# In the mixer of a two-layer transformer block, VectorE's normalisation of the attention probabilities moves in front of the low half of the weights

## The chip, the cores and the metric

The kernel runs on one core of one Trainium2 chip. The metric is the device time of one execution in microseconds (us); of several executions the median is given.

## The reference

Two blocks are computed one after the other for 256 tokens of width 2048, all in float32. The first block is a hybrid mixer (pooling, forgetting attention, a gated linear recurrence) and a gated feed-forward part, both modulated by a conditioning vector. The second block has two layers, and the change is in these. A layer is:

```python
h = rmsnorm_2(x, norm_mix[l]);  proj = h @ w_in[l]          # 2048 -> 4352: q, k, v of three kinds
oa = window_attention(...)         # 8 heads "A", bias from a table, a sink
ob = neighborhood_attention(...)   # 8 heads "B", bias, column mask
oc = axial_global_attention(...)   # 16 heads "C", rotary, normalised q and k
mix = concatenate([rmsnorm_2(oa, ga), rmsnorm_2(ob, gb), rmsnorm_2(oc, gc)])
x = x + mix @ w_o[l]
u = relu(rmsnorm_2(x, norm_mlp[l]) @ w_up[l]);  x = x + (u * u) @ w_down[l]
```

In every head, `p = softmax(s)` over 256 keys and `o = p @ v`, for 256 queries and a head width of 64.

## The kernel before

**Weights in pieces.** All weights come as pieces of 512 rows by 512 columns (1 MB), 536 of them in the program, into a ring of four buffers. A float32 product is made of three products of rounded parts, so each piece goes through three hands: SyncE loads it into `raw` (`load`, L590), ScalarE rounds it into `w_hi` (`hi`, L2216 to L2218), VectorE makes the remainder `w_lo = raw - w_hi` (`lo`, L1263 to L1266). TensorE then does 48 matmuls of 256 columns on it (`piece`, L700, matmuls at L695). SyncE's load of a piece waits until TensorE has finished the piece four before (`pe_done`).

**One program of pieces.** In a layer of the second block, pieces 0 to 31 are `w_in`, 32 to 47 are `w_o`, and then comes the feed-forward part. Each engine has a loop over the pieces of its own, and a table of hooks: work that the engine does at a given piece, in the order in which it was registered. VectorE's loop is at L2112 to L2115: at step p it first makes `w_lo` of piece p + 1, then runs the hooks of p. ScalarE's loop casts `w_hi` of piece p + 1 at its step p and then runs its hooks. TensorE executes piece p and then its hooks of p. Semaphores tie the engines together. Each engine executes in order.

**Attention beside the pieces.** The 32 heads of a layer are spread over hooks by `head_slots` (L135 to L153), which gives for each p from 12 to 40 three lists of heads: those whose probabilities are transposed, those whose output is then computed, and those whose scores are computed. TensorE does all three as its hook of p (`slot`, L920; transposes at L698 in `turn`, in `finish`, L847, which waits for `p_done`). Starts are at 12, 14, ... 25, 27 (B4, B5), 29 (B6, B7), 31 (B0, B1), 33 (B2, B3), 34 (A0, A1), 36 (A2, A3), 38 (A4, A5), 39 (A6, A7); the first head of a pair is transposed at p + 1, the second at p + 2, or both at p + 1 where the next start follows directly.

On VectorE the same table is registered twice, at L2076 for the heads whose probabilities are due (`probs`, L1635: the reciprocal at L1648 and two multiplications at L1652, for A heads an addition at L1641 before them) and at L2082 for new heads (`row_max`, L1655: bias at L1677, mask at L1681, maximum at L1685 or L1687). Both are hooks of p + 1, so TensorE's transposes in its hook of p wait for VectorE's step p + 1. ScalarE computes the exponentials (`exps`, L2424) in its step p + 2 of the start and copies the transposed probabilities out of PSUM (L2389).

Other work of VectorE in this part: evacuations of projected tiles (`evac2`, L2020), sums of squares for the group norms (`fold`, L1317), reciprocal roots (`rsqrt`, L1271 to L1301), the norms (`group_norm`, L1993, and `group_lo`, L2002) and the residual sums (`add_plain`, L2007). GpSimd loads the bias tiles (L2789, L2795) into four buffers, each when the head four before has used its own.

Of the kernel before, what the change touches and what calls it, by code (L numbers as in the profile page):

```python
# [50 lines left out]
HEADS1 = 8  # L51
# [147 lines left out]
def width2(p):  # L199

    return 256 if p < 4 * len(IN2) and IN2[p // 4] == 7 else PIECE_N
# [52 lines left out]
HEADS2 = 32  # L254


def two_stage_kernel(nc, a, stage=9):

    with ExitStack() as ctx:
# [973 lines left out]
        def _(dve):  # L1233
# [4 lines left out]
            def hook(p, fn, *args):  # L1238
                hooks.setdefault(p, []).append((fn, args))

            def run_hooks(p):
                for fn, args in hooks.pop(p, []):
                    fn(*args)
# [19 lines left out]
            def lo(quad, j, n=PIECE_N):  # L1263
                dve.wait_ge(hi_done, quad * 4 + (j + 1))
                m = PIECE_K * n
                v.tensor_tensor(w_lo[j][:, 0:m], raw[j][:, 0:PIECE_K * n], w_hi[j][:, 0:m], ALU.subtract).then_inc(lo_done, 1)  # L1266
# [37 lines left out]
            def fold(bufs, start, sems, lo=0, hi=5, count=folded):  # L1304

                n = start + lo
                if lo == 0:
                    dve.wait_ge(*sems[0])
                acc = bufs[0]
                parts = [(acc[:, :, :], b[:, :, :], w) for b, w in zip(bufs[1:], sems[1:])]  # L1310
                parts += [(acc[:, 0:2, :], acc[:, 2:4, :], None), (acc[:, 0, :], acc[:, 1, :], None)]
                for k, (a_, b_, w) in list(enumerate(parts))[lo:hi]:
                    if w is not None:
                        dve.wait_ge(*w)
                    if k:
                        dve.wait_ge(count, n)
                    v.tensor_tensor(a_, a_, b_, ALU.add).then_inc(count, 1)  # L1317
                    n = n + 1
# [316 lines left out]
            def probs(H, kind, h, no):  # L1635

                b = H % 2
                dve.wait_ge(exp_done, no + 1)
                if kind == "A":
                    n = lay[0] * 40 + (HEADS1 + 24 + 2 * (H - 24))  # L1640
                    v.tensor_tensor(rsum[:, b, :], rsum[:, b, :], sink_e[:, b, :], ALU.add).then_inc(rcp_done, 1)  # L1641
                    dve.wait_ge(rcp_done, n + 1)
                    n = n + 2
                elif kind == "F":
                    n = H + 1
                else:
                    n = lay[0] * 40 + (HEADS1 + H + 1)
                v.reciprocal(rinv[:, b, :], rsum[:, b, :]).then_inc(rcp_done, 1)  # L1648
                dve.wait_ge(rcp_done, n)
                for t in range(QT):  # L1650
                    w = P * (t + 1) if kind == "F" else T
                    i = v.tensor_scalar(s_sb[b][:, t, 0:w], s_sb[b][:, t, 0:w], rinv[:, b, t:t + 1], None, ALU.mult)  # L1652
                i.then_inc(p_done, 1)
# [43 lines left out]
            def slot(done, new, base):  # L1697
                for H, kind, h in done:
                    probs(H, kind, h, base + H)
                for H, kind, h in new:  # L1700
                    row_max(H, kind, h, base + H)
# [217 lines left out]
            if stage >= 3:  # L1919
                mb = MISC_B  # L1920
                for l in range(LAYERS):
# [127 lines left out]
                    def fold_f(lo_, hi_):  # L2049
                        fold(sq_x, 0, [(sq_f, q + 1) for q in range(4)], lo_, hi_, folded_f)  # L2050

                    for q in range(1, 4):
                        hook(q - 1, split_lo, q, q, LC_MIX, nb)
                    fb = l * FOLD_L + FOLD_L0
# [19 lines left out]
                    for z in (24, 25):  # L2074
                        hook(Q_ALT_AT + 1, q_end, z)
                    for p, (done, _, _) in SLOTS2.items():  # L2076
                        hook(p + 1, slot, done, [], l * HEADS2 + HEADS1)
                    for z, p in Q_ROT_AT.items():
                        hook(p + 1, q_end, z)
                    for b_ in (1, 2):  # L2080
# [29 lines left out]
                    hook(52, read_rstd, "mlp")  # L2110

                    for p in range(48):  # L2112
                        if p:
                            lo(lq + (p + 1) // 4, (p + 1) % 4, width2(p + 1))
                        run_hooks(p)  # L2115
# [75 lines left out]
        def _(act):  # L2191
# [248 lines left out]
            for p, (_, _, new) in SLOTS1.items():  # L2440
                hook(p + 2, exps, new, 0)
            for p, (trans, _, _) in SLOTS1.items():
                hook(p + 1, copy_probs, trans, 0)
# [14 lines left out]
            for p, (_, outs, _) in SLOTS1.items():  # L2458
                hook(p + 1, copy_out, outs)
# [366 lines left out]
```

## Time and profile before

| | |
|---|---|
| median of 3 runs | 3362.93 us (3355.77 to 3363.58) |
| the profiled execution | 3361.67 us, span 3360.0 us |
| TensorE matmuls | busy 3233.0 us, 96% of the span |
| VectorE | busy 2225.3 us, 66% |
| ScalarE | busy 1420.0 us, 42% |
| mean granted TensorE clock | 0.972 |

The span is the time from the first to the last instruction in the profile; the device time has 1.67 us around it. In the names of engines, PE is TensorE, PEld its weight loads, DVE is VectorE, ACT is ScalarE, POOL is GpSimd and SP is SyncE. "G" and "Dn" are the accumulators in PSUM; scores, transposes and small products use the buffers of Dn. `s_sb` holds a head's scores and then its probabilities. Pieces 28 to 41, where the change works, lie at about 1426 to 1556 us of the span in layer 0 and at about 2478 to 2606 us in layer 1.

### The profile page before, as it was taken

What the parts mean: (1) busy time and instruction counts of PE and PEld (TensorE: products, weight loads), DVE (VectorE), ACT (ScalarE), POOL (GpSimd) and SP (SyncE); (2) the same over time, 40 slices, a digit from 0 to 9 for tenths busy, and PEclk for the clock granted to TensorE, in tenths of its full rate; (3) what the DMA queues carried; (4) which work ended last, traced back from release to release, by engine and by line L of the source; (5) the groups of instructions that cost most, each with busy time, mean ns of one, the idle gap of its engine ahead of it and who ended that gap; (6) DMA issues with size and microseconds to landing.
All of it is one profiled execution on the core that took longest, in us unless ns stands there. A gap on an engine that the chain in (4) does not pass through costs nothing.

```text
span 3360.0 us, 62992 instructions
## 1 busy us (share of the span) xinstructions
PE 3233.0 (96%) x27070; PEld 3157.3 (94%) x27070; DVE 2225.3 (66%) x2257; ACT 1420.0 (42%) x1384; POOL 158.1 (5%) x292
## 2 busy tenths in 40 slices
PE   5999979999999999989999999999999999999998
PEld 5988879999999999978999999999987999999998
DVE  5788877665666677677655555657667755555655
ACT  3243334444444444545433434334455434334333
POOL 2111100000000100011000000000010000000000
PEclk6899989999999999999999999999999999999999
DMA  9788867666666645445555555555444565555553
GB/s 385 283 307 310 293 256 253 220 211 213 208 204 205 220 151 164 140 138 163 188 195 192 192 195 189 198 189 175 139 138 139 176 197 190 194 193 190 197 189 136
DMA packets 320748, 681.66 MB, mean 203 GB/s; under 512 B 14769, under 2 KB 21621, under 8 KB 320165
## 3 DMA queue, kind: packets, MB, share of 16 engines
q1 hardware_dynamic: 286272, 562.74, 50.6%
q0 software_dynamic: 31232, 109.07, 8.9%
q10 hardware_dynamic: 3108, 7.89, 0.6%
q8 instruction: 104, 1.70, 0.2%
q14 instruction: 32, 0.25, 0.0%
HBM read 677.47 MB, written 7.94 MB: 204 GB/s over the span
## 4 chain that ended last, share of the span: by engine, by line
PE 84%; DVE 9%; DMA 3%; issue 2%; ACT 2%; POOL 0%; ACTq 0%; DVEq 0%; POOLq 0%; SPq 0%
PE G L695 51%; PE Dn L695 32%; DVE w_lo L1266 2%; DVE ada_acc L1393 1%; PE Dn L698 1%; DMA ada_raw<-in_w_ada 1%; DMA raw<-in_w_in 1%; DMA zT<-in_w_ada 1%; ACT w_hi L2218 1%; DVE sq L1317 1%; DMA raw<-in_w_out 0%; DVE s_sb L1677 0%; DVE sq L1993 0%; DVE s_sb L1681 0%; DVE s_sb L1652 0%
## 5 line engine op out<-in xcount | busy, mean ns | idle before, releaser
L2218 ACT CAST w_hi<-raw 128x2048 fp32r<-128x2048 f32 (+2 forms) x536 | 1017.3, 1900 | 1427.7 <-DMA raw<-in_w_down 428.6
L1266 DVE TENSOR_TENSOR w_lo<-raw,w_hi 128x2048 fp32r<-128x2048 f32 (+2 forms) x536 | 1219.4, 2275 | 603.0 <-ACT w_hi L2218 602.2
L695 PE MATMUL G<-h_hi,w_hi 128*128 128x256 f32 x5632 | 1583.5, 281 | 10.5 <-DVE w_lo L1266 6.3
L695 PE MATMUL G<-h_lo,w_hi 128*128 128x256 f32 x5632 | 1572.1, 279 | 0.0
L695 PE MATMUL G<-h_hi,w_lo 128*128 128x256 f32 x5632 | 1571.4, 279 | 0.0
L695 PEld LDWEIGHTS G<-h_hi,w_hi 128*128 128x128 f32 x5632 | 1071.2, 190 | 25.1 <-issue 20.8
L695 PEld LDWEIGHTS G<-h_lo,w_hi 128*128 128x128 f32 x5632 | 1071.4, 190 | 0.2
L695 PEld LDWEIGHTS G<-h_hi,w_lo 128*128 128x128 f32 x5632 | 1071.2, 190 | 0.0
L695 PE MATMUL Dn<-act_hi,w_hi 128*128 128x256 f32 x2752 | 763.0, 277 | 7.4 <-DVE act_lo L1811 7.4
L695 PE MATMUL Dn<-act_hi,w_lo 128*128 128x256 f32 x2752 | 762.5, 277 | 0.0
L695 PE MATMUL Dn<-act_lo,w_hi 128*128 128x256 f32 x2752 | 762.4, 277 | 0.0
L695 PEld LDWEIGHTS Dn<-act_hi,w_hi 128*128 128x128 f32 x2752 | 519.6, 189 | 7.9 <-DVE act_lo L1811 7.9
L695 PEld LDWEIGHTS Dn<-act_lo,w_hi 128*128 128x128 f32 x2752 | 519.4, 189 | 0.0
L695 PEld LDWEIGHTS Dn<-act_hi,w_lo 128*128 128x128 f32 x2752 | 519.3, 189 | 0.0
L2007 DVE TENSOR_TENSOR xT<-xT,Dn 128x1024 f32<-128x1024 f32 x128 | 156.4, 1222 | 171.3 <-PE Dn L695 171.2
L1393 DVE SCALAR_TENSOR_TENSOR ada_acc<-ada_raw,c_sil,ada_acc 128x1024 f32<-128x1024 f32 x110 | 140.9, 1281 | 19.1 <-DMA ada_raw<-in_w_ada 13.1
L2389 ACT COPY pT<-Dn 128x512 f32<-128x512 f32 x64 | 37.5, 585 | 158.7 <-PE Dn L698 158.7
L2795 POOL DMA_DIRECT2D bias<-rpb_rep x64 | 39.1, 620 | 1305.6 <-DVE s_sb L1677 1303.9
L1838 DVE TENSOR_TENSOR y_ff<-y_ff,Dn 128x1024 f32<-128x1024 f32 x40 | 48.8, 1221 | 54.5 <-PE Dn L695 54.3
L2753 POOL DMA_DIRECT2D ada_raw<-in_w_ada x120 | 63.7, 531 | 326.6 <-DVE ada_acc L1393 265.1
L698 PE MATMUL Dn<-ident,s_sb 128*128 128x128 f32 x280 | 44.9, 282 | 28.0 <-DVE s_sb L1652 26.4
L2122 DVE SCALAR_TENSOR_TENSOR stage_p<-G,rstd 128x1024 f32<-128x1024 f32 x32 | 39.2, 1225 | 47.7 <-PE G L695 47.6
(273 smaller groups left out, 1748.4 us busy)
## 6 DMA issues: line engine op xcount, KB each, us to landing
raw<-in_w_up SPq DMA_DIRECT2D x128, 1024.0 KB, 5.3
raw<-in_w_down SPq DMA_DIRECT2D x128, 1024.0 KB, 5.0
raw<-in_w_in SPq DMA_DIRECT2D x88, 1024.0 KB, 5.3
ada_raw<-in_w_ada POOLq DMA_DIRECT2D x120, 512.0 KB, 6.6
raw<-in_w_ffn_gate SPq DMA_DIRECT2D x44, 1024.0 KB, 5.1
raw<-in_w_ffn_up SPq DMA_DIRECT2D x44, 1024.0 KB, 5.1
raw<-in_w_ffn_down SPq DMA_DIRECT2D x44, 1024.0 KB, 5.0
raw<-in_w_o SPq DMA_DIRECT2D x32, 1024.0 KB, 5.0
```

The source lines that it names most:

```text
L695: return nc.tensor.matmul(o, lhsT, rhs, start=start, stop=stop, skip_group_check=True)
L698: return nc.tensor.transpose(o, i, ident[0:n, 0:n])
L1266: v.tensor_tensor(w_lo[j][:, 0:m], raw[j][:, 0:PIECE_K * n], w_hi[j][:, 0:m], ALU.subtract).then_inc(lo_done, 1)
L1317: v.tensor_tensor(a_, a_, b_, ALU.add).then_inc(count, 1)
L1393: x = v.scalar_tensor_tensor(out=acc[:, :], in0=w[:, :], scalar=c_sil[:, t:t + 1], in1=acc[:, :], op0=ALU.mult, op1=ALU.add)
L1838: v.tensor_tensor(y_ff[:, 4 * f:4 * f + 4, :], y_ff[:, 4 * f:4 * f + 4, :], buf[:, :, :], ALU.add)\
L2007: v.tensor_tensor(xT[:, 4 * f:4 * f + 4, :], xT[:, 4 * f:4 * f + 4, :], buf[:, :, :], ALU.add)\
L2122: v.scalar_tensor_tensor(out=stage_p[:, :, :], in0=G[b][:, :, :], scalar=0.0, in1=rstd[:, :].unsqueeze(1).broadcast_to([P, 4, T]), op0=ALU ...
L2218: s.copy(w_hi[j][:, 0:PIECE_K * n], raw[j][:, 0:PIECE_K * n]).then_inc(hi_done, 1)
L2389: s.copy(pT[H % 2][:, :, :], PT).then_inc(pt_copied, 1)
L2753: gp.dma_start(ada_buf(slot)[:, :], wv[:, t, bass.ds(col0, ADA_N)]).then_inc(ada_loaded[slot], 16)
L2795: gp.dma_start(bias[sl][64 * (r % 2):64 * (r % 2) + 64, r // 2, :] .rearrange("p (r c) -> p r c", r=4), bass.AP(tensor=rpb_rep, offset=off ...
```

## The change

In VectorE's program, heads whose probabilities are due in hooks of steps 29 to 41 (slots p of 28 and more) are no longer hooks. They are kept in a table and normalised at the head of the step, before `w_lo` of piece p + 1 is made. The other slots stay as they are. The numbers of instructions on all engines stay the same, and so do the semaphores and their values.

```diff
@@ -2049,6 +2049,7 @@
+                    early = {}
                     for q in range(1, 4):
                         hook(q - 1, split_lo, q, q, LC_MIX, nb)
@@ -2074,7 +2075,10 @@
                     for p, (done, _, _) in SLOTS2.items():
-                        hook(p + 1, slot, done, [], l * HEADS2 + HEADS1)
+                        if p >= 28:
+                            early[p + 1] = done
+                        else:
+                            hook(p + 1, slot, done, [], l * HEADS2 + HEADS1)
@@ -2110,6 +2114,7 @@
                     for p in range(48):
+                        slot(early.get(p, []), [], l * HEADS2 + HEADS1)
                         if p:
                             lo(lq + (p + 1) // 4, (p + 1) % 4, width2(p + 1))
                         run_hooks(p)
```

## Rows read from the trace of the kernel before

**Rows 1.** The page: engines, busy time (share of the span) and instructions
```profile
PE 3233.0 (96%) x27070; PEld 3157.3 (94%) x27070; DVE 2225.3 (66%) x2257; ACT 1420.0 (42%) x1384; POOL 158.1 (5%) x292
```

**Rows 2.** TensorE's waits (total us, times, longest): whole span, 1425 to 1550, 2477 to 2600
```profile
PE Dn L698 <- DVE s_sb L1652: 26.4, 16, 4.0
...
PE Dn L698 <- DVE s_sb L1652: 13.3, 8, 4.0
...
PE Dn L698 <- DVE s_sb L1652: 13.0, 8, 4.0
```

**Rows 3.** Chain of waits behind piece 28 of layer 0 (start us, us, what)
```profile
1431.55 0.70 DVE sq L1317
1432.70 2.20 DVE w_lo L1266
1435.01 0.63 DVE s_sb L1652 x2
1435.68 1.12 PE Dn L698 x4
```

**Rows 4.** Timeline of TensorE, transposes that waited in layer 0 (start, us, [idle before])
```profile
1435.68 1.12 PE L698 MATMUL Dn<-ident,s_sb 128*128 128x128 f32 x4 [3.98 <-DVE s_sb L1652]
...
1456.58 0.66 PE L698 MATMUL Dn<-ident,s_sb 128*128 128x128 f32 x4 [2.31 <-DVE s_sb L1652]
...
1474.89 0.66 PE L698 MATMUL Dn<-ident,s_sb 128*128 128x128 f32 x4 [1.65 <-DVE s_sb L1652]
...
1491.13 0.66 PE L698 MATMUL Dn<-ident,s_sb 128*128 128x128 f32 x4 [1.67 <-DVE s_sb L1652]
...
1502.13 0.66 PE L698 MATMUL Dn<-ident,s_sb 128*128 128x128 f32 x4 [0.77 <-DVE s_sb L1652]
...
1509.73 0.66 PE L698 MATMUL Dn<-ident,s_sb 128*128 128x128 f32 x4 [1.04 <-DVE s_sb L1652]
...
1519.54 0.55 PE L698 MATMUL Dn<-ident,s_sb 128*128 128x128 f32 x3 [0.22 <-DVE s_sb L1652]
...
1527.34 0.66 PE L698 MATMUL Dn<-ident,s_sb 128*128 128x128 f32 x4 [1.68 <-DVE s_sb L1652]
```

**Rows 5.** Timeline of ScalarE and of VectorE around slot 35, layer 0
```profile
1499.82 0.19 ACT L2424 ACTIVATION_READ_ACCUMULATOR s_sb<-s_sb,negmax 128x1 f32 x1
...
1498.86 2.29 DVE L1266 TENSOR_TENSOR w_lo<-raw,w_hi 128x2048 fp32r<-128x2048 f32 x1 [0.64 <-ACT w_hi L2218]
```

**Rows 6.** Stretches: us, busy PE, PEld, DVE, ACT, POOL, clock, DMA share, GB/s; a gap
```profile
1433.80:1440.40 6.60, 4.72 (x22) 4.72 (x23) 4.40 (x16) 2.39 (x2) 0.00 (x0) 0.50 0.37 140
1457.80:1460.90 3.10, 3.10 (x17) 3.10 (x16) 2.07 (x2) 3.10 (x4) 0.00 (x0) 0.50 0.29 109
2489.00:2491.80 2.80, 2.80 (x15) 2.80 (x14) 2.56 (x10) 1.57 (x1) 0.00 (x0) 0.50 0.00 0
2509.00:2512.30 3.30, 3.30 (x18) 3.30 (x17) 2.36 (x2) 3.30 (x3) 0.00 (x0) 0.50 0.14 53
2526.10:2532.00 5.90, 5.90 (x51) 5.90 (x52) 2.85 (x4) 2.39 (x2) 0.00 (x0) 1.00 0.44 164
...
2526.00 0.66 PE L698 MATMUL Dn<-ident,s_sb 128*128 128x128 f32 x4 [1.86 <-DVE s_sb L1652]
```

**Rows 7.** Timeline: w_lo of piece 34 on VectorE, start of piece 34 on TensorE
```profile
1471.83 2.28 DVE L1266 TENSOR_TENSOR w_lo<-raw,w_hi 128x2048 fp32r<-128x2048 f32 x1
...
1483.75 0.38 PE L695 MATMUL G<-h_hi,w_hi 128*128 128x256 f32 x1
```

**Rows 8.** Timeline of VectorE: the first row maximum work after slot 36
```profile
1511.49 0.69 DVE L1677 SCALAR_TENSOR_TENSOR s_sb<-Dn,bias 128x512 f32<-128x512 f32 x1 [1.81 <-PE Dn L695]
```

**Rows 9.** DMA issues, 1420 to 1550 (out<-in, engine, count, KB each, us to landing)
```profile
raw<-in_w_o SPq DMA_DIRECT2D x13, 1024.0 KB, 5.0
bias<-rpb_rep POOLq DMA_DIRECT2D x32, 64.0 KB, 2.4
bias<-t_rep POOLq DMA_DIRECT2D x16, 128.0 KB, 2.6
```

## The prediction

> **What bounds the kernel now.** I read the page first. TensorE is busy for 96% of the span and VectorE for 66% [rows 1], so the time is what TensorE executes plus what it waits; the table of waits says for whom. The largest single line of TensorE's waits in the whole program is the one for the normalised probabilities of L1652, 26.4 us in 16 waits; asked for two stretches alone, the same table gives 13.3 us in 8 waits in layer 0's mixer and 13.0 us in 8 in layer 1's [rows 2]. That is all 16: this wait occurs nowhere else, and both stretches lie in pieces 28 to 38 of a mixer, where the change works. (By "slot p" I mean what TensorE does behind piece p: transposes of a head, scores, outputs.)
>
> Then the chain of waits shows why the probabilities are late. Behind piece 28 it goes: fold on VectorE, w_lo on VectorE (2.20 us until the next instruction starts), L1652, and only then TensorE's transposes at 1435.68 [rows 3]. The exponentials that L1652 needs are no part of it. So for 2.20 us VectorE makes the low half of piece 30 while TensorE, which has finished piece 28, stands still and could not use that half anyway: piece 29 comes first. The timeline of TensorE gives the size of each of the eight gaps of layer 0: slots 28, 30, 32, 34, 35, 36, 37, 38 [rows 4]. With eight waits counted and eight shown, the slots between have none.
>
> **The change, step by step.**
>
> Nothing is added or removed: the 16 heads from slot 28 on (B4 to B7, B0 to B3, A0 to A7) have the same instructions, in front of w_lo instead of behind it. No DMA is issued by either. VectorE's own work is unchanged.
>
> *Gaps.* Probabilities start 2.20 us earlier [rows 3] wherever their exponentials are done. A gap g shrinks by the smaller of g and 2.20:
> - slot 28: 3.98 - 2.20 = 1.78 stays; gain 2.20. Check: the fold lets go at 1432.70, reciprocal and two multiplications take as long as now (1435.68 - 2.20 - 1432.70 = 0.78), transposes at 1433.48.
> - slot 30: 2.31 - 2.20 = 0.11 stays.
> - slots 32, 34, 35, 36, 37, 38: 1.65 + 1.67 + 0.77 + 1.04 + 0.22 + 1.68 = 7.03, all gone.
> Layer 0: 13.3 - 1.78 - 0.11 = 11.4 us [rows 2, 4]. Layer 1 has the same eight waits with the same longest, 4.0: 13.0 less the same 1.9 is 11.1. Together **22.5 us**.
>
> The doubtful slot is 35, where the exponentials come late: those of A0 end at 1499.82 + 0.19 = 1500.01, while w_lo starts at 1498.86 [rows 5]. Now VectorE waits for them instead of using that time. The sink's addition, reciprocal and multiplications took about 1.0 (from w_lo's release to 1502.13 is 1502.13 - 1498.86 - 2.20 = 1.07), so transposes at 1501.08; piece 35 ends at 1502.13 - 0.77 = 1501.36 [rows 4, 5]. The gap goes, with 0.3 to spare.
>
> *Clock.* The half-clock stretches in this part are no accident of the piece. The granted clock is 0.50, the 1.2 GHz level, over 4.72 us of busy TensorE after the gap of 3.98, 3.10 after that of 2.31, and 2.80 and 3.30 in the same places of layer 1; after a gap of 1.86 in layer 1 the next piece runs at 1.00, 2.4 GHz [rows 6]. The gaps left are 1.8 and 0.1, both under 1.86, so I expect all four half-clock stretches to go. They hold 4.72 + 3.10 + 2.80 + 3.30 = 13.9 us. At half clock 18 matmuls stand in 3.30 us, at full clock 51 in 5.90 [rows 6]: 5.5 against 8.6 per us, so 0.37 of the time comes back, 5.1 us; by the two clock levels alone it is half, 7.0. I take **6 us**, the middle; the lower end is nothing, if the gap left behind piece 28 and the small matmuls around it still pull the clock down.
>
> The Trainium skill speaks against counting on this: TensorE: Matmul & The Clock Gate, section "A second HAM failure mode: psum-queue depth-cycling", says that frequent short idles between groups of matmuls are enough to make the clock go to and fro. By that rule the half-clock stretches stay and the sum is the one of the first rival below; the row after the 1.86 us gap disagrees, for one such gap.
>
> *w_lo, now later.* It ends some 0.8 us later against VectorE's previous work (up to 1.6 where a slot has two heads). Who waits for it: the piece after next on TensorE. The tightest case in layer 0 is piece 34: its w_lo starts at 1471.83 and takes 2.28, and the piece starts at 1483.75, 9.6 us later [rows 7]. Take off 1.65 for the gap that goes and 0.8 for the move, and 7 us remain. Cost nothing; if that cover were gone each slot would give its whole gain back.
>
> *Row maxima, behind the later w_lo.* Today VectorE idles 1.81 us after the probabilities until the next scores are there [rows 8]. Now a w_lo of 2.20 fills that idle, so where a slot scores new heads, their row maxima start some 0.4 us late (0.8 in slot 34, whose first scores come sooner). They feed ScalarE's exponentials, which mostly stand behind the cast of w_hi anyway, and then probabilities that now have 1 us or more in hand. I charge nothing; seven such slots in two layers at 0.45 would be 7 x 2 x 0.45 = 6.3 us if none were covered.
>
> *Queues.* GpSimd's loads of bias wait for the row maxima's first instruction, so they go out up to 0.8 later and land in 2.4 to 2.6 us [rows 9]; the slot they fill is read four heads on, more than 8 us later. SyncE's loads follow finished pieces, so they go out earlier with TensorE; 1 MB lands in 5.0 us [rows 9], under one piece's 5.9 us [rows 6].
>
> After the mixer TensorE is the bound again, so nothing gives the gain back. Sum against the profiled execution: 3361.67 - 22.5 - 6 = 3333.2. That execution is 1.3 us under the median of the runs (3362.93), well inside their spread of 7.8. Forecast **3333 us**, 0.9% faster.
>
> **The rivals.**
>
> *The clock does not come back* (chance 0.16). The gap behind piece 28 is only halved, and short idles of other kinds stay around it. Then only the gaps count: 3361.7 - 22.5 = 3339. For it: 1.8 is close to 1.86, and four matmuls of one column follow the transposes. Against it: the full clock after the 1.86 gap.
>
> *Exponentials become what ends the wait* (0.09). In the A heads, ScalarE's chain (output copy, square, cast of w_hi, exponentials) ends last and VectorE, in order, now sits in front of w_lo until it does. The A slots 35 to 38 keep their gaps, 0.77 + 1.04 + 0.22 + 1.68 = 3.7 per layer, 7.4 in all, so 3333 + 7.4 = 3341; with the late row maxima uncovered as well (6.3), 3347. Against it: the 0.3 us in hand in slot 35, and more elsewhere.
>
> *The transposes were waiting for something else, too* (0.03), the slower side. They also need the previous head's copy out of PSUM by ScalarE and its buffer. If that is what ended the gaps, they stay, and the later row maxima add their 6.3 us: 3361.7 + 6.3 = 3368. It decides as soon as an earlier L1652 does not bring earlier transposes. Against it: in slot 28 the transposes start 0.04 us after L1652's end (1435.01 + 0.63) [rows 3].
>
> *It does nothing that reaches the end* (0.04): the moved heads are not those that are waited for, or a later stage waits for a transfer instead and returns the gain; about 3361. Against it: the eight slots found are all from 28 on, and a load lands in less than a piece.
>
> **How the numbers follow.** The forecast itself has 0.68. Its best case: both full clock levels' worth (7.0), all 26.4 us of waits, since slot 28's neighbours may shift, makes 3361.7 - 26.4 - 7.0 = 3328; the spread of a median takes it to 3325. The upper end takes in the first two rivals to 3346. About 0.3%, 10 us, is what a measurement of this kernel can tell from no change, so "faster" means under 3353: 0.68 + 0.16 + 0.09, with a bit taken off for the unforeseen, 0.92. Same 0.05, slower 0.03.
>
> **What the profile of the changed kernel would show.** Right: TensorE's waits for L1652 fall from 26.4 us to under 5, in two waits of about 1.8 behind piece 28 of each layer; on VectorE, L1652 starts directly after the fold in that slot, and w_lo follows it; no stretch at 0.50 near pieces 29 and 31; no wait of a piece on w_lo. TensorE's busy time falls by some 6 us with the clock, the rest of the gain is idle time. Wrong: waits for L1652 that now end on exponentials (VectorE idle before L1641 or L1648 and TensorE idle with it), half-clock stretches still in place, or a new wait G on w_lo.

## The result and the profile after

| | before | after |
|---|---|---|
| median, first comparison | 3363.22 us (4 runs, 3355.77 to 3363.58) | 3321.98 us (4 runs, 3317.21 to 3324.82) |
| ratio | | 0.988, 95% interval 0.9865 to 0.9896 |
| profiled execution, span | 3360.0 us | 3319.9 us |
| TensorE busy, mean granted clock | 3233.0 us, 0.972 | 3212.5 us, 0.978 |

The changed kernel is 41 us faster; the forecast was 30, and its range ended 3 us above the measured median. In the table of waits of the changed kernel, the line that stood at 26.4 us in 16 waits [rows 2] is down to 4.0 us in 4, two in each layer:

```profile
PE Dn L698 <- DVE s_sb L1652: 4.0, 4, 1.8
```

The chain of waits behind piece 28 answers to [rows 3]: w_lo is gone from it, and the reciprocal starts where the fold ends.

```profile
1427.62 0.42 DVE sq L1317
1428.05 0.09 DVE rinv L1648
...
1428.16 0.63 DVE s_sb L1652 x2
...
1428.83 0.66 PE Dn L698 x4
```

TensorE's timeline of the changed kernel answers to [rows 4]: slots 28 (gap 1.78), 30 (gap 0.22), 32 and 35 of layer 0. The last two carry no idle time any more, and neither do 34, 36, 37 and 38.

```profile
1428.83 0.66 PE L698 MATMUL Dn<-ident,s_sb 128*128 128x128 f32 x4 [1.78 <-DVE s_sb L1652]
...
1445.28 0.66 PE L698 MATMUL Dn<-ident,s_sb 128*128 128x128 f32 x4 [0.22 <-DVE s_sb L1652]
...
1459.84 0.60 PE L698 MATMUL Dn<-ident,s_sb 128*128 128x128 f32 x4
...
1484.14 0.60 PE L698 MATMUL Dn<-ident,s_sb 128*128 128x128 f32 x4
```

Stretches of the changed kernel, with the columns of [rows 6]: behind the gap of slot 28, then from the start of piece 28 to that of piece 41, layer 0 and layer 1. The clock is 1.00, 2.4 GHz, in all three.

```profile
1428.80:1435.40 6.60, 6.57 (x56) 6.57 (x57) 6.25 (x16) 2.39 (x2) 0.00 (x0) 1.00 0.42 155
1421.10:1527.70 106.60, 102.87 (x831) 92.32 (x829) 91.55 (x168) 60.41 (x119) 28.12 (x48) 1.00 0.55 172
2454.80:2561.30 106.50, 102.77 (x830) 92.27 (x829) 91.27 (x168) 60.37 (x120) 18.10 (x32) 1.00 0.50 162
```

The same two stretches of the kernel before:

```profile
1425.80:1549.60 123.80, 108.76 (x831) 96.85 (x829) 92.25 (x168) 60.36 (x119) 28.13 (x48) 0.96 0.47 148
2477.60:2600.60 123.00, 108.23 (x830) 96.11 (x828) 92.07 (x168) 60.37 (x119) 18.35 (x32) 0.97 0.44 141
```

To the hundredth: 123.79 to 106.55 and 123.02 to 106.54 us, a gain of 17.24 and 16.48, together **33.7 us**. VectorE works as long as before (92.25 and 91.55); TensorE's busy time falls by 5.9 and 5.5. Of the 40.1 us between the two spans, 33.7 lie in these stretches and 6.4 outside, where both kernels execute the same instructions; 4.7 of those are gone before piece 28 of layer 0. The experiments had to say what these 6.4 us are and what makes up the 33.7.

### The profile page after: what moved, and what is told of

It reads as the page before. It is cut to its first block, busy times and chain, and to the rows that moved or that the text cites. A ratio compares the mean times of both kernels' runs of the same rounds, so it can differ in the third digit from the quotient of the medians.

```text
span 3319.9 us, 62992 instructions
## 1 busy us (share of the span) xinstructions
PE 3212.5 (97%) x27070; PEld 3139.8 (95%) x27070; DVE 2223.9 (67%) x2257; ACT 1420.3 (43%) x1384; POOL 157.6 (5%) x292
## 4 chain that ended last, share of the span: by engine, by line
PE 86%; DVE 7%; DMA 3%; issue 2%; ACT 2%; POOL 0%; ACTq 0%; DVEq 0%; POOLq 0%; SPq 0%
PE G L695 53%; PE Dn L695 33%; DVE w_lo L1266 2%; DVE ada_acc L1393 1%; PE Dn L698 1%; DMA raw<-in_w_out 1%; DMA raw<-in_w_in 1%; ACT w_hi L2223 1%; DMA zT<-in_w_ada 1%; DVE sq L1317 1%; DMA ada_raw<-in_w_ada 0%; DVE sq L1993 0%; DMA raw<-in_w_ffn_up 0%; DVE sq L1333 0%; DVE s_sb L1681 0%
## 5 line engine op out<-in xcount | busy, mean ns | idle before, releaser
L1811 DVE TENSOR_TENSOR act_lo<-stage_p,act_hi 128x1024 fp32r<-128x1024 f32 x43 | 52.4, 1219 | 6.4 <-ACT act_hi L2514 6.4
```

Source lines behind the costliest of these rows:

```text
L1811: v.tensor_tensor(act_lo[:, :, :], stage_p[:, :, :], act_hi[:, :, :], ALU.subtract).then_inc(a_lo, 1)
```

## The experiments

I use one measure throughout: TensorE's time from the first matmul of piece 28 to the first of piece 41 (the same two matmuls in every kernel, found by their number in order; the expectations say loosely "28 to 42" or "28 to 41"), and what is left around it. All numbers are in us, and the stretches come from one profile each. "Between" is the time from the end of layer 0's stretch to the start of layer 1's. A "pass" is one layer's stretch in one profile.

| kernel | to piece 28, layer 0 | stretch, layer 0 | between | stretch, layer 1 | rest | median, and of before beside it |
|---|---|---|---|---|---|---|
| before | 1425.8 | 123.8 | 928.0 | 123.0 | 759.4 | |
| changed | 1421.1 | 106.55 | 926.8 | 106.5 | 758.9 | 3321.98, 3363.22 |
| before again | 1422.0 | 125.7 | 928.3 | 123.1 | 758.9 | 3359.40, 3361.25 |
| changed again | 1427.6 | 108.3 | 927.6 | 106.7 | 759.0 | 3326.90, 3361.25 |
| slots 28 to 30 only | 1424.4 | 120.0 | 926.6 | 117.2 | 758.8 | 3347.04, 3361.25 |
| from slot 31 only | 1429.8 | 113.9 | 926.2 | 114.2 | 758.7 | 3337.67, 3361.25 |
| layer 0 only | 1422.9 | 108.3 | 927.8 | 123.1 | 759.1 | 3343.19, 3361.20 |
| evacuation later | 1423.9 | 105.6 | 927.8 | 105.3 | 759.1 | 3322.26, 3361.20 |
| all slots | 1426.9 | 108.3 | 927.5 | 106.7 | 759.2 | 3328.46, 3361.20 |
| more work (16 bytes in the middle) | 1437.2 | 111.1 | 943.9 | 110.8 | 775.2 | 3378.91, 3361.20 |
| more work (16 bytes at the end) | 1420.3 | 110.3 | 927.8 | 110.3 | 757.7 | 3329.27, 3361.33 |
| 16 bytes, no work | 1433.4 | 106.9 | 944.3 | 106.7 | 776.9 | 3374.49, 3361.33 |
| 64 bytes, no work | 1434.5 | 106.1 | 945.7 | 108.2 | 776.6 | 3372.13, 3361.33 |

### Both kernels again

No edit. Expected of the kernel before:

> The kernel of before once more, to see what a second execution of the same instructions does outside the stretch of the change. The two profiles so far differ by 4.7 us before piece 28 of layer 0, where both kernels have the same instructions, and by 6.9 us in all outside pieces 28 to 41. Theory A (chance of the execution: stretches at half clock in the first 1300 us fall where they fall): this profile reaches piece 28's start anywhere within 5 us of the first one's 1425.8, and the ratio to the kernel before is 1.000. Theory B (something of the program: the same instructions always take the same time there): it reaches it within 1 us of 1425.8.

Expected of the changed kernel:

> The changed kernel once more. Theory A (4.7 us early was chance): it reaches piece 28 of layer 0 anywhere within 5 us of 1421.1, and the median over more rounds comes out 33 to 36 us under the kernel before (what lies in pieces 28 to 41 of both layers), ratio 0.9895 to 0.990. Theory B (the change also speeds up what lies outside): 39 to 42 us, ratio 0.988.

Measured: ratio 0.9991 (0.9979 to 1.0002) for the kernel before, whose own runs reach from 3349.6 to 3370.6 us over both sets. It reached piece 28 after 1422.0 us, 3.8 earlier than its first profile; the changed kernel reached it after 1427.6, 6.5 later than its first. So theory A holds: the 4.7 us are of the size by which a profile of the same kernel differs from itself, and the second pair even had it the other way round. The 6.5 is more than the 5 that the expectation allowed. The ten profiles with the same buffers lie between 1420.3 and 1429.8. The changed kernel was 34.4 us faster this time, ratio 0.9887 (0.9871 to 0.9903): its median is inside what theory A gave (33 to 36), though the ratio, whose interval spans both theories, would not decide it. The stretches do.

The second profile of the kernel before held something that I had not seen: a ninth gap. Its timeline of TensorE, slot 31 of layer 0:

```profile
1461.67 0.66 PE L698 MATMUL Dn<-ident,s_sb 128*128 128x128 f32 x4 [1.57 <-DVE s_sb L1652]
```

In this execution piece 31 ran at full clock (5.69 us from its first matmul to the end of its last, where the first profile had 7.42), and then its transposes stood waiting for the same thing. In the first profile the slow piece had covered this wait: from the transposes of slot 30 to those of slot 31 both profiles took 8.10 us, one with a slow piece and no wait, the other with a fast piece and a wait.

### The change in two parts

```diff
-                        if p >= 28:
+                        if 28 <= p <= 30:
```

> Only the heads of slots 28 to 30 (B4, B5, B6) are normalised first; from slot 31 on w_lo is first again. If the gaps of 3.98 and 2.31 us are what pulls the clock down, this part gives 2 x (2.2 + 2.2) = 8.8 us of gaps and all of the clock's 7 to 8 us, together 16 to 17 us, and no stretch at 0.50 within 30 us behind piece 28. If the clock does not hang on these two gaps: 8.8 us and the half-clock stretches stay.

```diff
-                        if p >= 28:
+                        if p >= 31:
```

> Only the heads from slot 31 on are normalised first; slots 28 to 30 as before. Gaps only: 2 x 7.0 us plus about 0.1 for each of 12 starts that no longer wait, 15 to 16 us, with both half-clock stretches of each layer still there. If the parts simply add, this and the run with slots 28 to 30 alone make up the gain of the whole change, 32 to 34 us; if the clock needs both, they make less.

Measured: 14.2 us and 23.6 us by the medians; by the stretches 3.8 + 5.8 = 9.6 and 9.9 + 8.8 = 18.7. In slots 28 to 30 alone the clock comes back for piece 31, and the wait of slot 31 comes out in its place, as its timeline shows: VectorE has w_lo before the reciprocal again, and TensorE waits 1.34 us (1.56 in layer 1). From the transposes of slot 30 to those of slot 31 it took 8.09 us in both layers, as in the kernel before; with the whole change it takes 6.38.

```profile
1455.10 2.29 DVE L1266 TENSOR_TENSOR w_lo<-raw,w_hi 128x2048 fp32r<-128x2048 f32 x1 [0.39 <-ACT w_hi L2223]
1457.31 0.16 DVE L1648 RECIPROCAL rinv<-rsum 128x2 f32<-128x2 f32 x1
...
1458.18 0.65 PE L698 MATMUL Dn<-ident,s_sb 128*128 128x128 f32 x4 [1.34 <-DVE s_sb L1652]
```

My expectation for this part missed that (16 to 17), and its "no stretch at 0.50": in layer 0 the clock fell behind slot 28, and once more behind slot 38, after a gap of 1.69 us:

```profile
1522.30:1525.50 3.20, 3.20 (x16) 1.65 (x13) 2.57 (x5) 0.73 (x2) 1.25 (x2) 0.50 0.56 193
```

The second part came out above its 15 to 16. Its table of waits shows 26.4 - 12.8 = 13.6 us less wait, 5.1 less than the stretches gained. About 1 us of this is the clock: it did not fall behind slot 30 in layer 0, where the expectation had the half-clock stretch stay (worth 1.7 us), and behind slot 28 of that layer more of the slow time fell on matmuls instead of on the gap (0.7 us lost). The other 4 us are waits that were worth more than the idle time shown.

```profile
PE Dn L698 <- DVE s_sb L1652: 12.8, 4, 4.0
```

Do the parts add? The stretches give 28.3 where the whole change has 33.7. Of the 5.4 us missing, 1.8 is the wait of slot 31 in layer 1, which the second part meets behind a slow piece and the first part uncovers. The rest is the clock in layer 0, which in these two profiles fell behind slots 28 and 38 or cost more behind slot 28, and did not fall in the first profile of the changed kernel. The medians give 37.8 where the whole change has 41.2 in one comparison and 34.4 in the other, so they show no shortfall. Only the covered wait is shown; how far the parts add is not.

### Layer 0 alone

```diff
-                        if p >= 28:
+                        if p >= 28 and l == 0:
```

> The change in layer 0 alone. In the three profiles of the two kernels the stretch from piece 28 to piece 42 goes from 123.8 to 106.6 us in layer 0 and from 123.0 to 106.5 in layer 1. If the layers are independent, this kernel has 106.5 to 108.3 in layer 0 and 123.0 to 125.7 in layer 1, and its median lies 17 us under the kernel before, ratio 0.995. If the gain reached beyond the stretch, more than 17 and a different time between the two stretches than 926.8 to 928.3 us.

Measured: ratio 0.995 (0.9935 to 0.9965), 18.0 us; stretches 108.3 and 123.1, 927.8 between them. The layers are independent, and nothing beyond chance is gained or returned outside.

### The rest of the wait in slot 28

```diff
                     for p in range(48):
                         slot(early.get(p, []), [], l * HEADS2 + HEADS1)
+                        if p == 29:
+                            evac2(6)
...
-                        hook(4 * g + (4 if g else 5 if l else 6), evac2, g)
+                        if g != 6:
+                            hook(4 * g + (4 if g else 5 if l else 6), evac2, g)
```

> The changed kernel, with the evacuation of the seventh group (L2020, 1.21 us, and its mark, 0.15) taken from in front of the fold of group C to behind the probabilities of slot 28. If the wait of 1.78 us left in slot 28 is VectorE's order alone, it falls by 1.35 to 0.43 us in both layers: 2.7 us, and less again where the clock no longer falls there (it fell in one of four passes of the changed kernel, about 1.7 us each). 2.7 to 3.5 us under the changed kernel. If exponentials or the fold's input end the wait instead, it stays over 1 us.

Measured: the gap went from 1.78 to 0.65 in both layers. It is VectorE's order alone. Counted from the first matmul of piece 28 the transposes start 1.34 us earlier, as expected (after 7.70 us in the changed kernel, 6.36 here); the printed gap fell by only 1.13, another sign that it is not exact. The stretches are 105.6 and 105.3, so 1.0 and 1.2 shorter than the best of the changed kernel, a little less than the expected 2.7 in all. Its median, 3322.26, lies 4.6 under "changed again" and level with "changed": 2.2 us are shown by the profiles and not by the medians.

```profile
1430.21 0.66 PE L698 MATMUL Dn<-ident,s_sb 128*128 128x128 f32 x4 [0.65 <-DVE s_sb L1652]
```

### Normalising first in all slots

```diff
-                        if p >= 28:
+                        if p >= 12:
```

> The changed kernel, with the heads of slots 12 to 27 normalised first too, where TensorE waited for none in the kernel before. If an earlier normalisation only pays where TensorE waits for it, the time is that of the changed kernel within 1 us, waits for L1652 still 4.0 us in 4. If w_lo behind the probabilities has a price of its own, it shows here: up to 8 slots x 2 x 0.45 = 7 us slower.

Measured: 3328.46, 1.6 us over "changed again" at 3326.90, though 6.5 over the first median, so the medians do not decide. The time between the stretches does: it holds slots 12 to 27 of layer 1, and 927.5 lies between the 926.8 and 927.6 of the changed kernel. The waits for L1652 are 4.2 us. Where TensorE does not wait, the order makes neither a gain nor a price that can be seen here.

### How much VectorE could take

The edit adds 1.2 us of work per step, whose result is not used:

```diff
         rs_mark = sb("rs_mark", [P, 4])
+        junk = sb("junk", [P, 4])
...
+                        if 29 <= p <= 41:
+                            v.tensor_reduce(junk[:, 0:4], xT[:, 0:4, :], AX_X, ALU.max)
                         run_hooks(p)
```

> The changed kernel with one more instruction on VectorE in each of steps 29 to 41, a maximum over 1024 numbers (about 1.2 us) behind w_lo and in front of the row maxima, its result unused. It makes root, row maxima and everything behind later by 1.2 us more than the change did. Theory (the later w_lo and row maxima are covered by slack of about 1 us): 4 to 5 us for both layers, as new waits for L1652 of about 1 us in slots 36 and 38 only. Rival (VectorE is now the bound in this stretch): all of it comes out, 13 x 2 x 1.2 = 31 us.

Measured: 3378.91, slower than the kernel before by a ratio of 1.0054 (1.0034 to 1.0074). This looked like the rival and more, but the table shows where the time sits: 4.6 and 4.2 us in the stretches (each with one fall of the clock, worth 1.5), and 16 to 17 us each between and behind them, with some 10 us before, in parts *without* any added instruction. So I moved the 16 bytes behind `rot_q`, the last buffer, and in two more kernels left an unused buffer behind `rs_mark` (16 and 64 bytes) and took the instruction out:

> The additional instruction of r7 once more, with its 16 bytes of result placed behind all other buffers, so that no buffer of the kernel moves. Theory (r7's time outside the stretch, 16 us more in each feed-forward part, came from buffers moved by 16 bytes): outside as in the changed kernel (926.8 to 928.3 us between the stretches), inside 4 to 5 us more per layer than 106.5, as in r7 where a gap of 0.9 us stood in slots 32 and 36; median 8 to 10 us over the changed kernel, 3334 to 3337. Rival (the instruction itself costs outside too): 3375 to 3383 again.

> The changed kernel with an unused buffer of 16 bytes in the place where r7 had it, and no more instructions. Theory (the place of buffers): the stretches at 106.5 to 108.3, the time between them about 944 instead of 927, median 42 to 50 us over the changed kernel, 3368 to 3375, and matmuls on act_hi at a mean of 281 ns instead of 276. Rival (the instruction did it): as the changed kernel.

> The same unused buffer at 64 bytes. If what counts is where buffers start within a block of 64 bytes or less, nothing moves and the time is that of the changed kernel, 3322 to 3329. If any move costs: as with 16 bytes.

Measured: with the bytes at the end of the buffers, 3329.27 us, 2.4 over "changed again" and 7.3 over the first median (8 to 10 expected), and the usual times outside. Of the 13 x 2 x 1.2 = 31 us of added work 3.8 us per layer came out, 7.5 in all. The table of waits of layer 0's stretch shows them: the probabilities 3.8 instead of 2.0 (0.87 in slot 32, 0.96 in slot 36), and 1.0 for a buffer that the group norm (L1998) frees late, in slot 30. These are not the slots of the first expectation (36 and 38), and 7.5 us is more than its 4 to 5.

```profile
PE Dn L699 <- DVE s_sb L1653: 3.8, 4, 1.8
PE Dn L699 <- DVE rs_z L1998: 1.0, 1, 1.0
```

So behind the changed order most steps have more than 1.2 us in hand, and a few have less. With the bytes in the middle and no work, the stretches are those of the changed kernel and the loss outside is there in full, for 16 as for 64 bytes; the last expectation's first case, that 64 would be free, is refuted.

## Why the prediction was right or wrong

**The bound and the mechanism: right.** The 16 waits are where the rows put them, w_lo in front of the probabilities is what made them, and moving it took them away: forecast 1.78 left in slot 28 and 0.11 in slot 30, measured 1.78 and 0.22. Of 22.5 us of waits forecast, 26.4 - 4.0 = 22.4 went.

**The step that failed first: "A gap g shrinks by the smaller of g and 2.20", summed with the idle time shown. 22.5 us forecast, 26.5 measured.** The sum of the stretches is 33.7 and the clock's part 7.2 (next point), which leaves 26.5. Where the gap was longer than 2.20, the rule held: the transposes of slot 28 follow the first matmul of piece 28 after 9.90 us before and 7.70 now, and from piece 30 to piece 31 TensorE takes 8.84 before and 6.63 now. In the six other slots of layer 0, the time from the first matmul of the piece to the first of the next fell by 2.05, 1.87, 0.98, 1.21, 0.44 and 1.90, together 8.45; layer 1 gives the same to 0.02. The printed gaps are 7.03 in layer 0 and 6.6 in layer 1. That makes 3.2 us too little in twelve waits. The printed idle time is not the standstill: the wait of slot 32 is printed as 1.65 in layer 0 and 1.86 in layer 1, with 7.98 us from piece to piece both times, and it was worth 2.05. The timeline shows part of the reason: where the transposes do not wait, they start 0.16 us before the modelled end of the piece (1459.84 in slot 32, where that end is 1460.01). I had seen starts ahead of ends in the timeline and charged nothing for it. Another 0.8 us lies in slots 33, 39 and 40, where no wait was printed at all; why is open.

**The step "Clock": 6 taken, 7.2 measured.** From transposes to transposes, slot 28 to 29 took 8.84 and takes 6.60 in layer 0, 8.12 and 6.60 in layer 1; slot 30 to 31 took 8.10 and 8.09 and takes 6.38 and 6.37: 2.24 + 1.52 + 1.72 + 1.72. That is nearer to my upper bound (7.0 by the two levels) than to my middle. The two terms of 1.72 need the order of slot 31 as well: with slots 28 to 30 alone they were nothing. But the reason I gave, that a gap under 1.86 leaves the clock alone, is refuted. In the profiles of all kernels with 1.8 to 2.0 us left in slot 28 there are 17 passes through it, and in 7 the clock fell behind it; with the whole gap (3.98 to 4.2) it fell in 7 of 7, with 0.65 in 0 of 2. Behind slot 30 it fell in 5 of 7 passes with the whole gap (2.31 to 2.43) and in 0 of 19 with 0.1 to 0.2 left. "Changed again" has one of the seven, layer 0:

```profile
1436.60:1439.80 3.20, 3.20 (x17) 3.20 (x16) 2.85 (x14) 1.78 (x1) 0.00 (x0) 0.50 0.50 190
```

It costs the 1.7 us between its 108.3 and the 106.55 of the first profile. The first profile of the changed kernel escaped in both layers. And in the second profile of the kernel before it fell to 1.2 GHz after a gap of 1.86 in slot 32:

```profile
1472.80:1476.10 3.30, 3.30 (x17) 3.30 (x17) 1.09 (x1) 2.18 (x2) 0.00 (x0) 0.50 0.56 217
```

With the fall after 1.69 us in slot 38, shown above, these are the only two falls behind 24 gaps of 1.3 to 1.9 us outside slot 28. So the size of the gap alone does not decide, and slot 28 falls more often; what else it takes is open. The first rival, as a whole, is refuted, but what it describes happens in some passes. The Trainium skill fits this better than my threshold did: TensorE: Matmul & The Clock Gate, section "What's actually happening", says that the window over which activity is watched is free-running and "doesn't reset when your kernel starts", so the same gap may meet it well or badly. No run here shows that window itself.

**What I had left out: the covered wait.** Slot 31's wait of about 1.6 us, hidden in the first profile by piece 31 at half clock. It cost this forecast nothing, because the change removes it along with the others. A forecast that returned the clock without the order is 3 us too good; that is one part of why mine for slots 28 to 30 missed.

**The step that put the result outside the range: 3 us for "the spread of a median".** 33.7 us, taken from 3361.7, is 3328. My best case had 33.4 us and the same 3328, partly by luck: it counted 4.0 us of waits that stayed, and lacked the 4 us above. From there I allowed 3 us down to 3325, where ten profiles of unchanged code up to piece 28 lie 9.5 us apart, so the lower end should have been about 3318. The two first profiles differ by 6.4 us outside the stretches. In the second pair the changed kernel took 5.1 us more there than the kernel before, so these 6.4 are chance as far as the profiles show. Over both comparisons the changed kernel's nine executions have a median of 3323.8, 37 to 38 us under the kernel before; the 4 us over 33.7 are not located in any profile.

**The other rivals.** Exponentials do end one wait of VectorE: 1.83 us in slot 35, in front of L1641.

```profile
1482.98 0.16 DVE L1641 TENSOR_TENSOR rsum<-rsum,sink_e 128x2 f32<-128x2 f32 x1 [1.83 <-ACT s_sb L2429]
```

The probabilities are ready at 1483.38 + 0.62 = 1484.00 and TensorE goes on at 1484.14 without idle time: 0.1 to spare where I had worked out 0.3. Late row maxima and the later w_lo cost nothing measurable: none of the 13 times from one piece to the next, in either layer, is longer in the first profile of the changed kernel than in the kernel before, and TensorE waits for no w_lo in the stretch. Their slack is not large, though: another 1.2 us per step cost 3.8 us a layer. That the transposes waited for something else as well, and that a later stage takes the gain back, are both refuted: the transposes come as soon as the probabilities do, and the time between the stretches and the rest are the same, within 2 us, in every kernel whose buffers did not move.

## What to carry to other kernels

An engine's program may have work that nobody needs yet in front of work that the bounding engine waits for. Swapping the two takes away the wait, up to the length of what stood in front (2.20 us here), and where the wait is shorter than that it is worth 0.2 to 0.4 us more than the idle time that the profile prints. Count what a slow clock or another delay may cover: after such a repair the next wait in the same row of steps comes out. For a gain of 1%, take the spread from stretches that both kernels share before giving a range.

## What the runs showed that I had not expected

**Where buffers lie changed the time of matmuls.** An unused buffer of 16 bytes per partition, declared in the middle of the others so that all behind it moved, made the kernel about 50 us slower: 3374.49 against 3322.0 and 3326.9; 64 bytes did the same, 3372.13. The groups by line in 1700 to 2200 us (feed-forward part of layer 0) show which matmuls: those with `act_hi` and `act_lo`, which lie behind the new buffer, take a mean of 281 or 282 ns instead of 276, and those with `h_hi`, which lie in front of it, are unchanged. The changed kernel, then the one with 16 bytes:

```profile
L695 PE MATMUL Dn<-act_hi,w_hi 128*128 128x256 f32 x765 | 211.1, 276 | 0.0
...
L695 PE MATMUL G<-h_hi,w_hi 128*128 128x256 f32 x707 | 195.1, 276 | 0.0
```

```profile
L696 PE MATMUL G<-h_hi,w_hi 128*128 128x256 f32 x731 | 202.0, 276 | 0.0
...
L696 PE MATMUL Dn<-act_hi,w_hi 128*128 128x256 f32 x704 | 198.4, 282 | 0.0
```

At 5 to 6 ns over 3 x 2752 such matmuls that is 41 to 50 us, about the whole loss. The place fits too: the stretches, which hold no such matmul, are as long as ever. The same bytes behind the last buffer cost nothing. Which property of the address it is stays open: not a start at a multiple of 64 bytes, since 64 bytes keep that. In this kernel, an experiment that adds a buffer has to put it last, or it measures this as well.

**The same gap does not always have the same consequence for the clock,** as told above: 7 of 17.
